# Moving ScalarE's squares and VectorE's weight rests inside the attention pipeline of a two-block kernel

## The reference

```
h = rmsnorm(x) @ w_in                       # split into the queries, keys and values of three kinds
fox  (4 heads of 64):  softmax(q k / 8 + d) v,     causal, d a cumulated gate
diff (4 heads of 128): o1 = softmax(q1 k1 / 8 + alibi) v;  o2 = softmax(q2 k2 / 8 + alibi) v
                       o = rmsnorm(o1 - lam * o2, diff_norm_g) * (1 - lam_init)
mla  (4 heads of 64):  softmax(q k / sqrt(96)) v
x = x + concat(fox, diff, mla) @ w_o
```

## Time and profile before

| What | us |
|---|---|
| median of 3 runs | 2654.82 |
| lowest, highest | 2654.45, 2655.48 |
| time of the profiled execution | 2657.8 |
| span of the profiled execution | 2656.3 |
| TensorE busy in that span | 2577.5 (97%) |
| VectorE busy | 1172.7 (44%) |
| ScalarE busy | 896.3 (34%) |

### The profile page before, as it was taken

The page is one execution under the profiler, slowest core; times in us unless marked ns, Lnnn a source line. Parts: engine busy times, 40 slices in busy tenths (PEclk is TensorE's granted clock), DMA queues, the critical chain, the costliest instruction groups (busy, mean ns, idle before and its releaser), DMA issues.

```text
span 2656.3 us, 32800 instructions
## 1 busy us (share of the span) xinstructions
PE 2577.5 (97%) x13272; PEld 1790.4 (67%) x13276; DVE 1172.7 (44%) x2176; ACT 896.3 (34%) x1715; POOL 355.1 (13%) x162
## 2 busy tenths in 40 slices
PE   7999999999999999999999999999999999999999
PEld 6875444444777444444477678888888767888887
DVE  3543322332686223322355443562554544465264
ACT  4431111111483111111165454442345445443233
POOL 2200000000341000000021011221222001123212
PEclk9999999999999999999999999999999999999999
DMA  6229999999423999999932012322132111223212
GB/s 213 69 80 419 419 420 419 419 419 419 148 95 141 419 419 419 419 420 419 414 104 80 33 64 71 105 95 95 64 115 69 61 48 58 71 95 111 87 62 82
DMA packets 139033, 543.26 MB, mean 205 GB/s; under 512 B 18816, under 2 KB 30336, under 8 KB 89728
## 3 DMA queue, kind: packets, MB, share of 16 engines
q1 hardware_dynamic: 129264, 536.94, 51.7%
q10 hardware_dynamic: 9616, 4.18, 0.6%
HBM read 538.99 MB, written 2.10 MB: 204 GB/s over the span
## 4 chain that ended last, share of the span: by engine, by line
PE 90%; DVE 6%; ACT 2%; issue 1%; POOL 0%; DMA 0%; ACTq 0%; POOLq 0%; DVEq 0%
PE ps L615 23%; PE ps L1413 17%; PE ps L617 14%; PE ps L1435 8%; PE ps L1388 5%; PE ps L637 5%; PE ps L549 3%; PE ps L1450 3%; PE ps L1451 2%; PE ps L2017 2%; PE ps L550 1%; PE ps L1986 1%; PE ps L2008 1%; PE ps L467 1%; DVE w L279 1%
## 5 line engine op out<-in xcount | busy, mean ns | idle before, releaser
L615 PE MATMUL ps<-w,w 128*128 128x512 f32 x2976 | 680.5, 390 | 2.5 <-POOL w L279 2.5
L615 PEld LDWEIGHTS ps<-w,w 128*128 128x128 f32 x2976 | 559.1, 188 | 120.1 <-POOL w L279 3.4
L279 POOL TENSOR_TENSOR w<-w,w 128x1024 fp32r<-128x1024 f32 (+2 forms) x136 | 331.0, 2442 | 2169.9 <-ACT w L271 2165.6
L1413 PE MATMUL ps<-w,w 128*64 128x512 f32 x2048 | 451.6, 594 | 1.8 <-issue 1.8
L617 PE MATMUL ps<-w,w 128*128 128x512 f32 (+1 forms) x1872 | 408.0, 379 | 3.2 <-DVE w L535 3.0
L271 ACT ACTIVATE w<-w 128x1024 fp32r<-128x1024 f32 (+2 forms) x260 | 252.4, 999 | 413.5 <-PE ps L615 179.3
L617 PEld LDWEIGHTS ps<-w,w 128*128 128x128 f32 x1872 | 337.8, 188 | 69.7 <-issue 4.7
L279 DVE TENSOR_TENSOR w<-w,w 128x1024 fp32r<-128x1024 f32 (+2 forms) x124 | 210.6, 1705 | 380.9 <-ACT w L271 378.2
L1413 PEld LDWEIGHTS ps<-w,w 128*64 128x64 f32 x2048 | 146.1, 137 | 285.5 <-issue 285.5
L1674 DVE TENSOR_TENSOR X<-ps,X 128x512 f32<-128x512 f32 x256 | 162.3, 682 | 181.7 <-PE ps L1451 180.7
L1435 PE MATMUL ps<-w,w 128*64 128x512 f32 x1024 | 226.8, 595 | 0.8 <-ACT w L1502 0.8
(11 more groups left out here) (252 smaller groups left out, 2293.1 us busy)
## 6 DMA issues: line engine op xcount, KB each, us to landing
w<-in_moe_w_gate SPq DMA_DIRECT2D x128, 1024.0 KB, 15.9
w<-in_moe_w_up SPq DMA_DIRECT2D x128, 1024.0 KB, 18.4
w<-in_moe_w_down SPq DMA_DIRECT2D x128, 1024.0 KB, 15.4
w<-in_w_up SPq DMA_DIRECT2D x40, 1024.0 KB, 5.1
w<-in_w_down SPq DMA_DIRECT2D x20, 1024.0 KB, 5.2
w<-in_w_in SPq DMA_DIRECT2D x16, 1024.0 KB, 5.1
w<-in_ab_w_in SPq DMA_DIRECT2D x10, 1024.0 KB, 5.0
w<-in_c_w_in SPq DMA_DIRECT2D x8, 1024.0 KB, 6.9
```

Of the source, the lines that this page charges most:

```text
L279: up(self.wlo[self.low[s][0]], lane.e.tensor_tensor(lo, raw, hi.bitcast(F32), ALU.subtract))
L615: ins = pe.matmul(bank[:, :], wp[:, k, P * o:P * o + P], ap(k0 + k), start=first, stop=stop)
L1413: ins = pe.matmul(bank[64 * e:64 * e + 64, :], XG[p % 3][:, 4 * u + k, 64 * e:64 * e + 64], w[e][:, k, :], start=(u == 0 and k == 0), stop ...
```

## The change

1. ScalarE's 16 squares move into the run of the second kind: one at the end of a step, five steps behind the scores (four for the last block). `scalar_values`, which did nothing, becomes `scalar_squares_of_values`; a lag may now be a function of the job.
2. `diff_norm_g` is multiplied by 1 - lam_init once, at the start of the attention (128x128), and VectorE's four multiplications of 128x512 go. `o_done` is raised by each of the 16 tiles.
3. VectorE's `vector_turn` is cut up. In the second kind the reciprocals come one step behind the scores and after the maxima, the share at the end of that same step, and the mixture first in the next step. The scaling of the value products of the second kind comes four steps behind in place of three, except for its last four blocks.
4. In the first and the third kind the reciprocals keep their lag of 2, but stand after the maxima.
5. VectorE's two weight rests of `fv` move from step 2 of the third kind, behind the norm, to step 5, ahead of that step's two features.

```diff
-                for lag, part in engine:
-                    m = 2 * (p - lag)
-                    if 0 <= m < len(jobs):
-                        part(m0 + m, jobs[m:m + 2])
+                    for m in range(max(0, 2 * (p - 5)), min(2 * p + 2, len(jobs)), 2):
+                        if m // 2 + (lag(m0 + m) if callable(lag) else lag) == p:
+                            part(m0 + m, jobs[m:m + 2])
...
-            PE.wait_ge(o_done, 4)
+            PE.wait_ge(o_done, 4 * NT)
...
-        def scalar_values(m, two):
-            pass
+        def squares_lag(m):
+            return 5 if m < M_FOX - 2 else 4
+
+        def scalar_squares_of_values(m, two):
+
+            qc, kind, h = two[0][:3]
+            if kind == "diff0":
+                S.wait_ge(bo.free, turn_of(m) + 1)
+                up(sq, act.activation(SQ[:, 4 * qc + h, :], O[:, qc, 256 + P * h:384 + P * h], ACT.Square,
+                                      accum_out=SM[:, 64 + 4 * qc + h:65 + 4 * qc + h]))
...
-            engine = (2, scalar_turn), (0, scalar_scores), (3, scalar_values)
+            engine = (2, scalar_turn), (0, scalar_scores), (squares_lag, scalar_squares_of_values)
...
-            S.wait_ge(bo.free, turn_of(M_FOX))
-            for c in range(NT):
-                for h in range(4):
-                    up(sq, act.activation(SQ[:, 4 * c + h, :], O[:, c, 256 + P * h:384 + P * h], ACT.Square,
-                                          accum_out=SM[:, 64 + 4 * c + h:65 + 4 * c + h]))
...
-        def vector_turn(m, two):
+        def vector_reciprocals(m, two):
             V.wait_ge(bsc.free, m + 2)
-            n, i0 = P * (two[0][0] + 1), m % 8
+            i0 = m % 8
             up(rc, dve.reciprocal(AT[:, 16 + i0:18 + i0], AT[:, 8 + i0:10 + i0]))
+
+        def vector_share(m, two):
+
             if two[0][1] == "diff0":
                 V.wait_ge(nlam, 1)
                 V.wait_ge(rc, m // 2 + 1)
-                share = AT[:, 24 + i0:25 + i0]
-                vstep(dve.tensor_scalar(share, AT[:, 8 + i0:9 + i0], AT[:, 17 + i0:18 + i0], LS[:, 3:4], ALU.mult, ALU.mult))
-                up(mixed, dve.scalar_tensor_tensor(PB[m % 4][:, 0:n], PB[(m + 1) % 4][:, 0:n], share, PB[m % 4][:, 0:n],
-                                                   ALU.mult, ALU.add))
+                i0 = m % 8
+                up(share, dve.tensor_scalar(AT[:, 24 + i0:25 + i0], AT[:, 8 + i0:9 + i0], AT[:, 17 + i0:18 + i0],
+                                            LS[:, 3:4], ALU.mult, ALU.mult))
+
+        def vector_mixture(m, two):
+
+            if two[0][1] == "diff0":
+                V.wait_ge(share, (m - M_DIFF) // 2 + 1)
+                n = P * (two[0][0] + 1)
+                up(mixed, dve.scalar_tensor_tensor(PB[m % 4][:, 0:n], PB[(m + 1) % 4][:, 0:n], AT[:, 24 + m % 8:25 + m % 8],
+                                                   PB[m % 4][:, 0:n], ALU.mult, ALU.add))
+
+        def sums_lag(m):
+
+            return 1 if M_DIFF <= m < M_FOX else 2
+
+        def values_lag(m):
+
+
+            return 4 if M_DIFF <= m < M_FOX - 8 else 3
...
+            vstep(dve.tensor_scalar(dnB[:, i, :], dnB[:, i, :], 1.0 - lam_init, None, ALU.mult))
             V.wait_ge(lam_out, 1)
...
-            engine = (2, vector_turn), (0, vector_scores), (3, vector_values)
+            engine = (2, vector_mixture), (0, vector_scores), (sums_lag, vector_reciprocals), (values_lag, vector_values), (1, vector_share)
...
-                        ins = dve.scalar_tensor_tensor(o, o, SM[:, 64 + 4 * c + h:65 + 4 * c + h], dnB[:, i, :],
-                                                       ALU.mult, ALU.mult)
...
-                for c in range(NT):
-                    up(o_done, dve.tensor_scalar(O[:, c, 256:768], O[:, c, 256:768], 1.0 - lam_init, None, ALU.mult))
-
-            def norm_and_low():
-                norm_of_diff()
-                vector_product(("fv", i))
+                        up(o_done, dve.scalar_tensor_tensor(o, o, SM[:, 64 + 4 * c + h:65 + 4 * c + h], dnB[:, i, :],
+                                                            ALU.mult, ALU.mult))
+
+            def low_and_features(ks):
+                if ks == FEATURES_OUT[2:4]:
+                    vector_product(("fv", i))
+                vector_o_features(ks)
             two_kinds(engine, lambda: vector_product(("dv", i)), lambda: vector_product(("fqk", i)))
-            third_kind(engine, norm_and_low, vector_o_features)
+            third_kind(engine, norm_of_diff, low_and_features)
```

More of the change, by code:

```diff
@@ L1859, in program @@
     bsc, bpt, bo = handoff("scores"), handoff("turned"), handoff("values")
-    lam_in, lam_out, nlam, ckv, q1k1, mx, rc, mixed, o_done, cum, cum_parts = (
-        sig(n) for n in ("lam_in", "lam_out", "nlam", "ckv", "q1k1", "max", "recip", "mixed", "o_done", "cum", "cum_parts"))
+    lam_in, lam_out, nlam, ckv, q1k1, mx, rc, share, mixed, o_done, cum, cum_parts = (
+        sig(n) for n in ("lam_in", "lam_out", "nlam", "ckv", "q1k1", "max", "recip", "share", "mixed", "o_done", "cum", "cum_parts"))
     OUT_ORDER = (1, 0)
```

## The result

| | us |
|---|---|
| kernel before, median (lowest to highest) | 2655.4 (2654.45 to 2657.48), 11 runs |
| changed kernel, median (lowest to highest) | 2647.15 (2644.56 to 2650.6), 11 runs |
| ratio | 0.997, 95% interval 0.9963 to 0.9978 |
| predicted | 2646.3, range 2642 to 2651 |

What follows compares the result with a forecast made beforehand. TensorE, busy 97% of the span, was taken as the bound, so only its idle time and low clock count. 3.8 + 4.1 + 2.8 - 2.2 = 8.5 us off 2654.8 gave 2646.3 us, range 2642 to 2651.

Steps and rivals of the forecast that it cites:

- 3.8: Second kind's run: mixture first in its step shortens TensorE's waits for it, 1.9 us a layer, 3.8 us in all.
- 4.1: Third kind: moving the rests removes TensorE's wait before its first features, 2.2 + 1.9 = 4.1 us.
- 2.8: Third kind: the low clock behind the features' wait goes too, 1.4 us a layer, 2.8 us in all.
- 2.2: Third kind's step 5: the moved rests make TensorE wait 1.1 us a layer, a cost of 2.2 us.
- the two places: Second kind's run, where transposes wait for VectorE's mixture (6.2 us a layer), and third kind's steps 2 to 4 (2.17 us wait).
- The three waits of 0.34: TensorE's mixture waits in the run, due to VectorE's 0.43 us wait for value products; claimed to vanish, 3 x 0.34 a layer.
- 0.30 and 0.59: Run: lengths claimed to stay of TensorE's mixture waits of 0.41 and 0.70, each 0.11 us shorter.
- my 0.04: Run: offset in us between the TensorE and VectorE paths, used in sizing the waits of 0.41 and 0.70.
- Rival 1: Run gains nothing: VectorE's chain stays as long, or squares delay ScalarE's copies; 2650.1 us, chance 0.12.
- by themselves worth nothing: Squares and joined factors bring the norm forward about 4 us, but TensorE needs nothing of it then: 0 us alone.
- rival 4: Step 5: rests collide with GpSimd's again, pair takes 6.7 us, TensorE waits 5.4 a layer; 2657.7 us, chance 0.06.
- Rival 2: Clock falls elsewhere, at step 5's new wait or shifted waits, 3.5 us a layer at 1.2 GHz; 2649.1 us, chance 0.17.

Runs made afterwards that it cites:

- experiment 1: Changed kernel with VectorE's two weight rests back in step 2 of the third kind, behind the norm: 2641.62 us, ratio 0.9952 to the kernel before.
- experiment 2: Changed kernel with ScalarE's 16 squares as one block after the second kind's run again: 2645.81 us, ratio 0.9967 to the kernel before.
- Experiment 3: Kernel before with only the squares in the run and the joined factors; VectorE's order and rests as before: 2648.41 us, ratio 0.9978.
- experiment 4: Kernel before with only VectorE's two weight rests moved to step 5 of the third kind: 2648.05 us, ratio 0.9977.
- experiment 5: Kernel before with only VectorE's new order; squares a block, factors apart, rests at step 2: 2651.47 us, ratio 0.999.
- experiment 6: Changed kernel with reciprocals and share of the second kind's qc 1 and qc 0 blocks ahead of the next step's maxima: 2642.12 us, ratio 0.9957.
- experiment 7: Changed kernel with early reciprocals and shares and the rests back at step 2 together: 2639.41 us, ratio 0.9947 to the kernel before.
- experiment 8: Kernel of experiment 7 plus eight matmuls without use in the 2.46 us wait at the first kind's third step: 2637.66 us, ratio 0.9934.
- experiment 11: Kernel of experiment 7 timed again unaltered, on the chip of experiment 8: 2640.88 us, ratio 0.9944 to the kernel before.
- experiment 10: Changed kernel timed again unaltered, on the chip of experiment 8: 2646.49 us, ratio 0.9969 to the kernel before.

## Why the prediction was right, and where its terms were off

**The sum.** Forecast were 3.8 + 4.1 + 2.8 - 2.2 = 8.5 us. The stretches give 4.2 for the run, and 5.7 for the third kind, where 4.1 + 2.8 - 2.2 = 4.7 were forecast; 9.9 in all. The median moved by 8.25. So the two places are enough for the whole gain. That the clock elsewhere took back the 1.6 between them is not shown for the typical execution. On record are only mean clocks: 0.9947 over the changed kernel's 11 executions and 0.9945 over the 21 of the kernel before in experiments 1 to 4, so the typical execution gained next to nothing by its clock, where the two profiled third kinds gained 3.2 us. That the forecast lies within 0.3 us of the median is therefore in part luck.

**The run.** It gained 2.09 us a layer, 1.9 were forecast, and experiment 5 shows that VectorE's order alone does it. The three waits of 0.34 went, as forecast. The others were mis-sized: 0.42 and 0.77 stayed where 0.30 and 0.59 were forecast. VectorE's path was right (maxima at 1503.10, TensorE released at 1505.20, 2.10 us against 2.15 forecast). Wrong was the offset on TensorE's side: where it does not wait for its transposes it starts them at 1502.95, under the last matmul of the scores and 0.15 ahead of VectorE's maxima, so it arrives earlier at the next wait than I reckoned. The 0.59 has a slip besides: my 0.04 went into the two steps with opposite signs, and 2.15 against 1.52 less 0.04 is 0.67.

The total came out by luck in part. From start to start of the transposes, before and after, the step ahead of the wait of 0.34 became 0.50 shorter (2.62 to 2.12 us), where 0.34 were forecast. The steps ahead of the waits of 0.41 and 0.70, forecast at 0.11 each, changed by 0.04 and by -0.03 (2.42 to 2.38, 2.22 to 2.25). The step ahead of the qc 2 transposes, forecast at nothing, became 0.10 shorter (2.81 to 2.71). A head takes 9.46 us against 10.07, 0.61 less, where these terms promised 0.56, though its waits as shown shrank by 0.26 only.

A wait costs more than its bracket says, since the bracket begins at the end that the trace gives the matmul before, and a matmul that waits for nothing starts ahead of that end: the scores' last ends at 1502.83 + 0.29 = 1503.12, and the transposes behind it start at 1502.95, 0.17 earlier. That fits the waits that went whole: 0.34 was worth 0.50, and the 2.17 and 1.90 before the features 2.34 and 2.06 (first scores of step 2 to first features, 7.43 and 7.15 us before, 5.09 after). Rival 1 (the run gains nothing) fell; its argument, maxima to mixture still in line, was true, and experiment 6 took another 2.5 us a layer out of that line.

**The squares and factors.** Their step in the prediction failed, though the sum did not need it: "by themselves worth nothing". Experiment 3 gives 7.4 us for them alone, experiment 4 gives 5.7 for the moved rests alone, and the two together 5.7. It was one loss with two remedies. I had looked only at when the norm ends, and not at ScalarE's high halves, which the squares delay. With the squares in the run these halves are made one by one as `fv` proceeds, not three in a row; VectorE makes its first rest before GpSimd has one, and the collision of the earlier trace rows never happens. Given the squares, the moved rests only cost: 0.83 us a layer (experiment 1).

**The rests at step 5.** Forecast: 2.4 us for the pair, a wait of 1.1, 2.2 us in both layers. Measured: 2.35, and waits of 1.07 and 1.08. Their cost is 0.89 and 0.96 us (from the second features to the third, 3.91 and 3.84 us before, 4.80 after), as a short wait stood there before. The collision of rival 4 did not come: GpSimd has nothing there.

**The clock.** The low stretch behind the features went. I put 1.4 us a layer on it. From the first features to the second TensorE took 5.58 us in the first layer and 5.57 in the second, and takes 3.98 now: 1.60 and 1.59. That is the whole 1.6 of full-rate time that I had cut down to 1.4, so the cut was wrong. The third kind's terms are then 4.4 + 3.2 - 1.9 = 5.7 us. Rival 2 is partly true: a low clock followed the new wait at step 5 in 3 of the 10 profiled stretches that have this wait unfilled (experiment 2 first layer, experiment 6 both), at 1.5 to 1.6 us each, and in none of the 10 with the rests at step 2 (experiments 1, 3, 7, 8, 11). It is not in the profile of the changed kernel; whether it is in its slower executions no profile shows.

**Open.** The 6 us spread of the changed kernel goes with the clock: its three fastest executions (up to 2645.4 us) have a mean granted clock of 0.996, its two slowest (2650.5 and 2650.6) 0.994 and 0.993. An estimate from that: 0.002 to 0.003 of some 2645 us is 5 to 8 us. In which stretches the slow ones lost it is not known, since its two profiled executions (2644.65, and 2642.21 in experiment 10) are fast ones. The joined factors were never tested apart from the squares. And of experiment 1's lead over the changed kernel, some 3 us more than its stretches give have no shown cause.

## What to carry to other kernels

Before moving work off a place, ask which of the engines there is late, and for what: here two weight rests collided with another engine's, and either starting them earlier or moving them away removed the loss, so the second remedy added only its own price. Where a chain max, sum, share, mixture decides the pace, look for links whose inputs are a step old and put them where the engine waits for its next input; that gave 5 us here, more than the order it improved on. And check medians against stretches of the timeline between fixed rows: wherever the clock stayed high, the same order of work gave the same length to 0.11 us in both layers of every profile, while medians wandered by some us and shifted from one series to the next.

## What the runs showed of the hardware

A wait of 2.46 us on TensorE was followed by a low clock (granted 0.66 over 5 us in experiment 11) in 20 of 24 profiled cases, but not in all: the kernel before has it in the second layer and not in the first, with the same wait in both. It costs 1.67 us each time, and with eight matmuls without use in the wait the clock was 1.00 in both layers of the one profile. Even a wait of 1.08 us was followed by it in three cases of ten. And next to GpSimd's rests VectorE's two took 6.70 us, where they take 2.35 without them. Neither merely ran a little slower: the first took 3.40 us and ended at 1560.98, 1.08 behind GpSimd's first (1557.23 + 2.67), and the second ended 1.07 behind GpSimd's second.

```profile
1557.58 3.40 DVE L279 TENSOR_TENSOR w<-w,w 128x1024 fp32r<-128x1024 f32 x1
```
